# First and last norm of a two-model kernel: inputs in more loads, products of zeros on TensorE, sums and statistics in another order

## The reference, cut to what matters

```
def layer_norm(x, g, b):
    mu = mean(x); xc = x - mu
    var = mean(xc * xc)
    return xc * rsqrt(var + LN_EPS) * g + b

def reference(x, ...):
    h = layer_norm(x, ln_in_g, ln_in_b)          # "ln_in" in the kernel
    y = mixer_sublayer(h, ...)                   # begins with h @ w_in
    ...                                          # experts, the second model's first layer
    x = layer_norm_2(ALPHA * x + fox_mixer(x), ln_mix_g[1], ln_mix_b[1])           # "lnm1"
    x = layer_norm_2(ALPHA * x + conv_ffn(x, ...), ln_ffn_g[1], ln_ffn_b[1])       # "lnf1"
    return x
```

## Time and profile before

| | us |
|---|---|
| median of three runs | 2559.88 (2559.47 to 2563.92) |
| the profiled execution's own time | 2559.38 |
| its span in the trace | 2557.5 |
| TensorE busy in that span | 2515.7 |
| before the first matmul | 8.65 |
| first matmul to the first of `four_by_halves` | 12.93 |
| VectorE's first step behind the last tile (2543.09) to the end of the span | 14.4 |

### The profile page before, as it was taken

The page is one execution under the profiler, slowest core; times in us unless marked ns, Lnnn a source line. Parts: engine busy times, 40 slices in busy tenths (PEclk is TensorE's granted clock), DMA queues, the critical chain, the costliest instruction groups (busy, mean ns, idle before and its releaser), DMA issues.

```text
span 2557.5 us, 31104 instructions
## 1 busy us (share of the span) xinstructions
PE 2515.7 (98%) x10560; PEld 1874.6 (73%) x10560; DVE 1344.0 (53%) x2453; ACT 607.2 (24%) x1376; POOL 84.3 (3%) x117
## 2 busy tenths in 40 slices
PE   7999999999999999999999999999999999999998
PEld 6857767684444457888746888888885668888886
DVE  6787554351111136646385777753361857777633
ACT  3244112130000003222232322210231633222112
POOL 0010000000000010000020000000000100000000
PEclk9999999999999999999999999999999999999999
DMA  3224222248999952222112222223322012222233
GB/s 143 83 66 181 83 82 78 95 170 307 362 335 333 334 197 77 84 84 90 66 50 93 80 91 90 82 91 132 107 87 80 9 66 91 91 85 87 90 116 123
DMA packets 90382, 319.01 MB, mean 125 GB/s; under 512 B 9584, under 2 KB 13680, under 8 KB 90256
## 3 DMA queue, kind: packets, MB, share of 16 engines
q1 hardware_dynamic: 81408, 284.37, 32.2%
q10 hardware_dynamic: 5152, 19.92, 2.0%
q0 software_dynamic: 3728, 13.44, 1.6%
HBM read 295.61 MB, written 22.02 MB: 124 GB/s over the span
## 4 chain that ended last, share of the span: by engine, by line
PE 91%; DVE 4%; ACT 2%; issue 1%; DMA 1%; POOL 0%; ACTq 0%; POOLq 0%; DVEq 0%
PE bank L881 44%; PE bank L609 13%; PE bank L1071 13%; PE bank L853 4%; PE bank L989 3%; PE bank L733 2%; PE bank L755 1%; PE bank L1350 1%; PE bank L1338 1%; PE bank L1220 1%; PE bank L782 1%; ACT R L1474 1%; DVE R L2857 1%; PE bank L1083 1%; PE bank L643 1%
## 5 line engine op out<-in xcount | busy, mean ns | idle before, releaser
L881 PE MATMUL bank<-SQ,arena 128*128 128x256 f32 x2040 | 468.1, 379 | 0.0
L881 PEld LDWEIGHTS bank<-SQ,arena 128*128 128x128 f32 x2040 | 387.5, 190 | 52.8 <-DVE arena L2013 0.2
L1071 PE MATMUL bank<-arena 128*128 128x512 f32 x768 | 332.7, 592 | 0.8 <-ACT arena L1690 0.8
L881 PE MATMUL bank<-X,ring 128*128 128x256 f32 x1360 | 322.5, 379 | 0.0
L609 PE MATMUL bank<-arena,ring 128*128 128x256 f32 (+1 forms) x1280 | 319.5, 411 | 0.0
L609 PEld LDWEIGHTS bank<-arena,ring 128*128 128x128 f32 x1280 | 243.2, 190 | 74.9 <-issue 46.6
L881 PEld LDWEIGHTS bank<-X,ring 128*128 128x128 f32 x1360 | 258.2, 190 | 42.7 <-issue 8.4
L1071 PEld LDWEIGHTS bank<-arena 128*128 128x128 f32 x768 | 144.6, 190 | 176.5 <-issue 176.5
L2035 DVE TENSOR_TENSOR bank<-bank,arena 128x256 f32<-128x256 f32 x97 | 41.9, 432 | 242.1 <-ACT bank L1550 241.8
L881 PE MATMUL bank<-SQ,ring 128*128 128x256 f32 x680 | 160.8, 379 | 1.2 <-DVE R L2040 0.9
L881 PE MATMUL bank<-X,arena 128*128 128x256 f32 x680 | 160.7, 379 | 0.0
(11 more groups left out here) (367 smaller groups left out, 2950.7 us busy)
## 6 DMA issues: line engine op xcount, KB each, us to landing
ring<-w_stream SPq DMA_DIRECT2D x338, 512.0 KB, 3.3
arena<-w_stream SPq DMA_DIRECT2D x192, 512.0 KB, 5.1
y_slots<-X ACTq DMA_DIRECT2D x1, 9216.0 KB, 26.2
y_slots<-arena ACTq DMA_DIRECT2D x16, 512.0 KB, 5.1
X<-x_t SPq DMA_DIRECT2D x2, 1024.0 KB, 7.3
x_tok<-arena ACTq DMA_DIRECT2D x1, 2048.0 KB, 6.6
out_t<-X SPq DMA_DIRECT2D x16, 128.0 KB, 2.2
part<-params SPq DMA_DIRECT2D x1, 824.0 KB, 10.4
```

The lines of the kernel that those rows point to most:

```text
L881: mm = pe.matmul(out, w(n), v(k), start=start and n == 0, stop=n == len(chunk_pairs(p)) - 1, skip_group_check=not start)
L1071: mm = pe.matmul(ebank(t)[:, :], w_, ERING[:, at:at + S], start=(k == 0), stop=(k == len(lhs) - 1))
```

## The change

- **Loads.** The first half of `X` comes in three loads (chunks 0 to 3, 4 and 5, 6 and 7) with a semaphore each. The constants are put in another order, and the first 132 columns (`mean_d`, the two eps, zero, one) are loaded on their own, second in the queue. The other 1122 columns follow the second half of `X`.
- **Sums of the first norm.** `x_sums` makes two additions in place of three. The last pair of chunks is not added: `half_mean` multiplies it by `mean_d` directly, so that it has four matmuls in place of two.
- **Products of zeros.** VectorE first writes zeros into a part of `R`. TensorE multiplies them by themselves: 6 matmuls ahead of everything, 4 behind `half_mean` of half 0, and 4 behind `half_mean` of half 1, into a bank that is written afresh later.
- **Statistics.** `r_stats` takes the products in the order `SUM`, `SUMSQ`, chunk 7, chunk 7's square. On VectorE `add_square(6, 1)` moves ahead of `add_tile(7, 1)`. Both apply to all five norms.
- **Last norm by chunks.** For `lnf1`, half 1, two chunks are centred, then the reciprocal is taken, and then centring and scaling alternate by chunk.

The diff, cut to its core:

```diff
+NFIRST = CST0["ident"]
+X_PARTS = ((0, 0, 4), (0, 4, 6), (0, 6, 8), (1, 0, 8))
...
-            for h in range(2):
-                sp.dma_start(X[:, :, HALF[h]], x[:, HALF[h]].rearrange("(c p) s -> p c s", p=P))\
-                    .then_inc(x_loaded[h], 16)
-                if h == 0:
-                    sp.dma_start(cstt[:, :], cst).then_inc(constants_loaded, 16)
+            for n, (h, k0, k1) in enumerate(X_PARTS):
+                sp.dma_start(X[:, k0:k1, HALF[h]], x[k0 * P:k1 * P, HALF[h]].rearrange("(c p) s -> p c s", p=P))\
+                    .then_inc(x_loaded[n], 16)
+                if n == 0:
+                    sp.dma_start(cstt[:, 0:NFIRST], cst[:, 0:NFIRST]).then_inc(first_loaded, 16)
+            sp.dma_start(cstt[:, NFIRST:NCST], cst[:, NFIRST:NCST]).then_inc(constants_loaded, 16)
...
                 for n in range(2):
-                    mm = pe.matmul(abank(t)[:, 0:H], mean_d, half_sums(h)[:, n], start=(n == 0),
-                                   stop=(n == 1 and name == "ln_in"))
+                    pe.matmul(abank(t)[:, 0:H], mean_d, half_sums(h)[:, n], start=(n == 0), stop=False)
                 if name == "ln2":
                     a_read(pe, t - 1)
+                else:
+                    pe.wait_ge(x_loaded[2 + h], 16)
+                for n in range(2):
+                    mm = pe.matmul(abank(t)[:, 0:H], mean_d, LN[name]["src"][:, 6 + n, HALF[h]], start=False,
+                                   stop=(n == 1))
...
                 pe.matmul(abank(t)[:, 0:H], mean_d, SUM[:, HALF[h]], start=True, stop=False)
+                a_read(pe, t - 3)
+                pe.matmul(abank(t + 1)[:, 0:H], mean_d, SUMSQ[:, HALF[h]], start=True, stop=False)
                 m_read(pe, r_tile(name, 7, h))
                 pe.matmul(abank(t)[:, 0:H], mean_d, R[:, 7, HALF[h]], start=False, stop=True).then_inc(a_full, 1)
-                a_read(pe, t - 3)
-                pe.matmul(abank(t + 1)[:, 0:H], mean_d, SUMSQ[:, HALF[h]], start=True, stop=False)
...
-            pe.wait_ge(constants_loaded, 16)
+            def zeros_through(n):
+                for _ in range(n):
+                    pe.matmul(mbank(3)[:, 0:H], R[:, 7, 0:P], R[:, 7, 0:H], start=True, stop=True)
+
+            pe.wait_ge(warm, 1)
+            zeros_through(6)
+            pe.wait_ge(first_loaded, 16)
             half_mean("ln_in", 0)
+            zeros_through(4)
             half_mean_square("ln_in", 0)
             half_mean("ln_in", 1)
+            zeros_through(4)
+            pe.wait_ge(constants_loaded, 16)
             four_by_halves(T0["in"], "ln_in", {(0, 1): lambda: half_mean_square("ln_in", 1)})
...
+                add_square(6, 1)
                 add_tile(7, 1)
-                add_square(6, 1)
                 variance(1)
-                centre(1)
-                inverse(1)
-                scale(1)
+                if name == "lnf1":
+                    centre_chunk(0, 1)
+                    centre_chunk(1, 1)
+                    inverse(1)
+                    for k in range(C8):
+                        if k < C8 - 2:
+                            centre_chunk(k + 2, 1)
+                        if k == C8 - 1:
+                            a_read(dve, t0 + 3)
+                        else:
+                            dve.wait_ge(dve_step, step.now(1 if k + 2 < C8 - 1 else 0))
+                        scale_chunk(k, 1)
+                else:
+                    centre(1)
+                    inverse(1)
+                    scale(1)
...
             def x_sums(h):
-                dve.wait_ge(x_loaded[h], 16)
-                for j in range(1, 4):
...
+                dve.wait_ge(x_loaded[3 * h], 16)
+                step.inc(dve.tensor_tensor(half_sums(h), pairs(X, 0, h), pairs(X, 1, h), ALU.add))
+                if h == 0:
+                    dve.wait_ge(x_loaded[1], 16)
+                sync()
+                dve.tensor_tensor(half_sums(h), half_sums(h), pairs(X, 2, h), ALU.add).then_inc(half_summed, 1)
+
+            dve.memset(R[:, 7, 0:H], 0.0).then_inc(warm, 1)
             x_sums(0)
```

More of the change, by code:

```diff
@@ L96 @@
 PAR0, NPAR = starts(PAR, 1)
-CST = [("ident", 128), ("ones", 128), ("mean_p", 128), ("mean_d", 128), ("mask_fox", 128), ("mask_mla", 128), ("mask_ssd", 128), ("invcnt", 64),
+CST = [("mean_d", 128), ("ln_eps", 1), ("rms_eps", 1), ("zero", 1), ("one", 1),
+       ("ident", 128), ("ones", 128), ("mean_p", 128), ("mask_fox", 128), ("mask_mla", 128), ("mask_ssd", 128), ("invcnt", 64),
        ("before", 128), ("lane", 128), ("iota", NB + 1), ("tokens", 4),
-       ("invfreq", 1), ("sign", 1), ("ln_eps", 1), ("rms_eps", 1), ("zero", 1), ("one", 1), ("halfpi", 1)]
+       ("invfreq", 1), ("sign", 1), ("halfpi", 1)]
 CST0, NCST = starts(CST, 1)
+NFIRST = CST0["ident"]
+X_PARTS = ((0, 0, 4), (0, 4, 6), (0, 6, 8), (1, 0, 8))
 MIX = dict(ZB=0, ZP=6144, UP=8320, PW=10432, CQ=11488, CKV=13024, KT=14048, KR=15072, COS=15584,
@@ L173, in build @@
         a_out = [sem(f"a_out{i}") for i in range(4)]
-        constants_loaded, x_loaded = sem("constants_loaded"), [sem(f"x_loaded{h}") for h in range(2)]
+        constants_loaded, first_loaded, warm = sem("constants_loaded"), sem("first_loaded"), sem("warm")
+        x_loaded = [sem(f"x_loaded{n}") for n in range(len(X_PARTS))]
         loaded, p_loaded, sel_loaded = sem("loaded"), sem("p_loaded"), sem("sel_loaded")
@@ L661, in half_mean @@
                 for n in range(2):
-                    mm = pe.matmul(abank(t)[:, 0:H], mean_d, half_sums(h)[:, n], start=(n == 0),
-                                   stop=(n == 1 and name == "ln_in"))
+                    pe.matmul(abank(t)[:, 0:H], mean_d, half_sums(h)[:, n], start=(n == 0), stop=False)
                 if name == "ln2":
                     a_read(pe, t - 1)
-                    for n in range(2):
-                        mm = pe.matmul(abank(t)[:, 0:H], mean_d, R[:, 6 + n, HALF[h]], start=False, stop=(n == 1))
+                else:
[3 more added lines that the diff above has]
+                                   stop=(n == 1))
                 mm.then_inc(a_full, 1)
@@ L1523, in attention @@
                 outputs_of(n - 2)
-            act.wait_ge(constants_loaded, 16)
+            act.wait_ge(first_loaded, 16)
             act.activation(stat[:, 52:53], cm("one", 1), ACT.Sqrt, bias=cm("zero", 1))
@@ L2114, in variance, with centre_chunk @@
                     dve.engine_nop().then_inc(a_out[t % 4], 1)
+                def centre_chunk(k, h):
+                    t, cs = t0 + 1 + 2 * h, HALF[h]
+                    ins = dve.tensor_tensor(R[:, k, cs], R[:, k, cs], abank(t)[:, 0:H], ALU.subtract)
+                    if k < C8 - 1:
+                        step.inc(ins)
+                    else:
+                        ins.then_inc(a_out[t % 4], 1)
                 def centre(h):
-                    t, cs = t0 + 1 + 2 * h, HALF[h]
                     for k in range(C8):
[L2119 to L2123, removed]
+                        centre_chunk(k, h)
                 def inverse(h):
@@ L2127, in inverse, with scale_chunk @@
                     step.inc(dve.reciprocal(RSTD[:, HALF[h]], STD[:, HALF[h]]))
+                def scale_chunk(k, h):
+                    dve.tensor_tensor(R[:, k, HALF[h]], R[:, k, HALF[h]], RSTD[:, HALF[h]], ALU.mult)\
+                        .then_inc(r_scaled, 1)
                 def scale(h):
@@ L2132, in scale @@
                     for k in range(C8):
-                        dve.tensor_tensor(R[:, k, HALF[h]], R[:, k, HALF[h]], RSTD[:, HALF[h]], ALU.mult)\
-                            .then_inc(r_scaled, 1)
+                        scale_chunk(k, h)
                 def centre_tile(m, ready):
```

1 line of the change is left out of this document (added).

## The result

The changed kernel takes 2556.39 us (median of 18 runs), the kernel before 2562.43 in the 18 runs taken with it. Three of these 36 runs, at 3490, 4025 and 9535 us, lie far outside the rest and are left out of the ratio. The ratio is 0.9981, with an interval from 0.9974 to 0.9988 (the medians of the 33 runs that remain, 2556.27 and 2561.79, stand at 0.9978 to each other). In two later series the same pair gave 0.9978 (0.9969 to 0.9988) and 0.9968 (0.9956 to 0.9981), so the change makes the kernel faster by 0.2 to 0.3%. The profiled execution took 2554.69 us with a span of 2552.9; the one before had 2557.5.

The account below looks back on a forecast made before the run. TensorE was taken as the bound, busy 2515.7 of 2557.5 us, with gains only where it idles or runs slowly. 2559.38 - 3.8 - 2.05 = 2553.5 us, adjusted to 2553.7 for the base's median; range 2551.9 to 2557.2.

Parts of the forecast that it names:

- First load and additions: First norm: chunks 0 to 3 land at 4.95 us, 4 and 5 at 5.8, mean starts at 6.65.
- The range's lower end: Whole kernel: 2551.9 us, the low end of the forecast range.
- Zeros, clock, mean: First norm: zeros from 1.1 us raise the clock, mean takes 1.9 us, ready at 8.55 instead of 10.73; gain 2.2.
- the late rival: First norm: clock rises late or falls again, 1.7 to 1.9 us of gain lost, 2555.4 to 2557.3; chance 0.17.
- Mean square and behind it: First norm: mean square takes 1.9 us instead of 3.8, gain 1.9; loss 0.1 before the projection, near 17.6.
- Front in all: First norm: gains 2.2 and 1.9, loss 0.1, together 4.0 us, less 0.2 for the clock's rise; 3.8 counted.
- Zeros that do nothing: First norm: products of zeros do not raise the clock; 2559.8 us, no change, chance 0.05; slower variant chance 0.02.
- loads that land together: First norm: split load pieces all land at 6.5 us, mean starts 1.4 us later than forecast; 2555.1 us, chance 0.08.
- Tail: Last norm: statistics order gains 1.2 us, with chunks 2.05 us in all.
- The middle norms: Norms other than the last: statistics stand amid matmuls, so their new order is worth nothing.
- the sum's base: Whole kernel: 2559.38 us, from which gains are taken, with half of the profiled execution's 0.5 below median put back.
- no change that I held for less likely: Whole kernel: same within 0.2% (5.1 us), chance 0.31, against 0.65 for faster; line at 2554.8 us.

Follow-up runs that it names:

- e_fill: Changed kernel plus overwritten products in three more gaps (both attentions, ahead of the second model's first projection); 2554.52 us, ratio 0.9970 to the kernel before.
- e_first_only: Changed kernel with only the first group of six zero products, both groups of four dropped; single execution 2562.82 us.
- e_tail: Kernel before with only the new statistics order and the last norm by chunks; single execution 2559.13 us.
- e_chunks: Kernel before with only the last norm by chunks, statistics in their old order; single execution 2562.32 us.
- e_fill_before: Kernel before with only the three later gaps filled by products; the execution took 2561.61 us.
- e_loads: Changed kernel without any products of zeros; split loads, two additions, four-matmul mean and changed last norm stay; single execution 2558.97 us.

## Why the prediction was right and where it was wrong

*First load and additions.* Forecast: chunks 0 to 3 at 4.95, 4 and 5 at 5.8, the mean from 6.65. Found: 4.63, 6.12 and 6.95. The direction was right, the second load was 0.3 later. A slip stands in the first figure: 0.52 MB at 352 GB/s are 1.5 us, not 1.4, which gives 4.86. The load also varies: the second addition started between 5.70 and 7.15 over the kernels with split loads, and the projection followed it. The range's lower end counts 0.4 us for loads that land near 4 us. No run shows such a load: the first addition started between 4.42 and 4.69.

*Zeros, clock, mean.* Zeros from 1.18 (forecast 1.1), the clock up before the mean, eight records in 2.0 us (1.9). The gain of loads and mean was 1.77 where I had 2.2, the error being the second load (0.3) and a mean that took 0.1 longer. Of the five profiles with all three groups of zeros on split loads, none has zeros that do not raise the clock. In one (e_fill) it rose only during the mean, whose first four records took 1.36 us in place of 1.10: the late rival in a mild form, 0.3 us. That the clock needed both kinds of zeros I had seen only in part: I wrote that they lie hidden, not that without the groups of four the squares would be cold (e_first_only, 1.3 us).

*Mean square and behind it.* 1.79 (forecast 1.9) and a loss of 0.0 (0.1). Front in all 3.56, forecast 3.8. How near that came is partly luck: in the other four profiles with this front it was 3.98, 3.10, 3.50 and 2.64 us, by when the second load landed and, in e_fill, when the clock rose.

*The rivals.* Zeros that do nothing and loads that land together did not come true. The gap of 1.51 us between zeros and squares let the clock stay up in all five profiles.

*Tail.* 2.07, forecast 2.05. By its parts 1.12 and 0.95 in the profile after, 1.11 and 0.97 in the experiments.

*The middle norms.* Worth nothing, as forecast: the lead of 5.07 and later 5.6 us passes the first three unchanged.

**The step that failed is the sum's base, and with it the clock's falls, for which the sum has no term.** I put the 5.85 us against one execution of 2559.38 us and three runs, and added 0.25 for their median, which makes 2559.6. The kernel before takes 2562.4 to 2563.0 in the median of 18 to 20 runs, about 3 us more. In the first series 2.8 us from the base and 0.2 from the ends (5.63 in place of 5.85) make 3.0; the changed kernel's median of 2556.39 lies 2.7 above the forecast 2553.7. By the first ratio it would be at 0.9981 x 2562.43 = 2557.6, above my range's 2557.2, while its own median is within it. The change itself was forecast at 2553.7 / 2559.88 = 0.9976. The first series gave 0.9981, just on the side of no change that I held for less likely, the other two 0.9978 and 0.9968.

What I left out is that every profiled execution of either kernel loses clock somewhere in its middle, in places of which I had a row; I priced falls only for the start. In the 17 comparable runs of the changed kernel the time goes with the mean granted clock: 2552.44 us at 0.999, 2553.99 to 2555.79 at 0.998, 2554.68 to 2557.47 at 0.997, 2556.27 to 2559.01 at 0.996, 2563.22 and 2565.60 at 0.994. Single runs of one series spread over 8 to 13 us in this way, while medians of 8 to 20 runs repeat within 0.6. A base from three runs and one profile could be 3 us off for that alone.

*The kernel before can lose more than its profile showed.* e_tail, e_chunks and e_fill_before have its front and show a fall between 21.2 and 22.1, in the gap of 2.4 to 2.9 us ahead of the projection or right behind it. Three others with an open gap there have no fall: the profile before (2.2 us), e_loads (2.1) and e_first_only (2.0). In the eight profiles with products of zeros ahead of the projection that gap is closed to 0.3 us or less, and none has a fall there. That adds about 1.3 us to the gain in executions that have the fall (e_tail, 8.83 us in place of 7.50), and may be why the medians lie 6.0 to 7.1 us apart where the ends are worth 5.6. How often it happens was not measured.

## What to carry to other kernels

Cheap products on data that is already there, put into the gaps of a TensorE-bound program, can buy back the clock: here both the group ahead of the first real product and the groups between dependent ones were needed, and each was worth 1.3 to 1.6 us. Filling three later gaps took their falls away, but no shorter time was shown, and a filling longer than its gap delays what stands behind it. Splitting a load so that work starts earlier paid only together with that, because the extra matmuls it asked for ran at the lower clock otherwise. Before a change of 0.2% is summed against a kernel's time, take the spread of that time and its cause from many executions; a single profile fixes the parts, not the base.

## What the runs showed of the hardware that I had not expected

- The granted clock falls in a program that keeps TensorE 98% busy. It fell behind idle gaps of 1.23 us (second attention, seven of ten profiles), 1.63 (first attention, two of ten) and 2.00 (ahead of the second model's first projection, two of ten). In the two profiles that were compared a fall cost 1.5 and 3.0 us.
- It falls without idle time too. In the stretch from 520 to 560 us TensorE is busy for 40.00 of 40 us, with many products of 16 columns, and the clock's mean is 0.83 to 1.00 from one execution to the next.
- Products of zeros raise the clock as real ones do: it rose among the twelve of them, with nothing else on the engine.
- Of loads issued one behind the other the first landed within 0.3 us over the executions (additions from 4.42 to 4.69), the second within 1.5 (5.70 to 7.15).
